# Bias tables, weight rounding and the split of h moved in a two-block transformer kernel

## What is computed

```python
h = h + rms_norm(ffn, g_ffn_post[i])
e = rms_norm(p[i] @ w_ple_proj[i], g_ple[i])
h = h + jax.nn.sigmoid(h @ w_ple_gate[i]) * e
```

## Time and profile before

| | |
|---|---|
| median of 3 runs | 2031.25 us |
| the profiled execution's own time | 2030.91 us |
| its span | 2028.9 us |
| PE busy (share of the span) | 1913.7 us (94%) |
| DVE, ACT, POOL busy | 50%, 36%, 37% |
| mean granted TensorE clock | 0.962 of full speed |

### The profile page before, as it was taken

One profiled execution on the slowest core, in us unless ns is written; L12 is line 12 of the kernel. 1 busy time (PEld: TensorE's weight loads), 2 busy tenths in 40 slices (PEclk: granted clock), 3 DMA queues, 4 the chain that ended last, 5 costly groups with the idle time before them and its releaser, 6 DMA issues.

```text
span 2028.9 us, 25065 instructions
## 1 busy us (share of the span) xinstructions
PE 1913.7 (94%) x9252; PEld 1556.2 (77%) x9252; DVE 1016.7 (50%) x1695; ACT 736.6 (36%) x1233; POOL 753.9 (37%) x319
## 2 busy tenths in 40 slices
PE   7689899999999799999999999999788899999997
PEld 6577587788888677788888888888655588888886
DVE  6964558634444644235443335631587635334444
ACT  5175653322223341133222223332388733222221
POOL 4132043444444334353455444544100035444542
PEclk9799999999999899999999999988789999999999
DMA  5112032233333223873333332333001123332321
GB/s 192 31 63 63 1 98 79 83 104 104 93 93 104 63 71 104 143 190 104 104 91 106 98 98 83 104 96 96 27 22 32 53 73 102 95 101 85 94 93 62
DMA packets 52235, 177.52 MB, mean 87 GB/s; under 512 B 5527, under 2 KB 5911, under 8 KB 52152
## 3 DMA queue, kind: packets, MB, share of 16 engines
q1 hardware_dynamic: 47952, 166.22, 26.4%
q10 hardware_dynamic: 4200, 10.15, 3.4%
HBM read 166.88 MB, written 9.47 MB: 87 GB/s over the span
## 4 chain that ended last, share of the span: by engine, by line
PE 78%; issue 9%; DVE 8%; ACT 2%; POOL 2%; DMA 0%; DVEq 0%; POOLq 0%; ACTq 0%
PE ps L401 24%; PE ps L403 24%; PE ps L402 24%; POOL WL L370 2%; DVE arena L1515 2%; DVE arena L2072 1%; DVE arena L2055 1%; PE ps L840 1%; PE ps L513 1%; PE ps L817 1%; PE ps L805 1%; ACT arena L1346 1%; ACT arena L993 0%; PE ps L831 0%; ACT arena L1352 0%
## 5 line engine op out<-in xcount | busy, mean ns | idle before, releaser
L370 POOL TENSOR_TENSOR WL<-raw,WH 128x1024 fp32r<-128x1024 f32 x295 | 735.8, 2509 | 1207.8 <-ACT WH L891 1207.8
L401 PE MATMUL ps<-XH,WH 128*128 128x512 f32 (+1 forms) x1280 | 504.6, 394 | 48.7 <-DVE arena L1499 16.8
L402 PE MATMUL ps<-XL,WH 128*128 128x512 f32 (+1 forms) x1280 | 502.1, 392 | 0.0
L891 ACT ACTIVATE WH<-raw 128x1024 fp32r<-128x1024 f32 x295 | 303.8, 1053 | 545.9 <-PE ps L403 487.6
L403 PE MATMUL ps<-XH,WL 128*128 128x512 f32 (+1 forms) x1280 | 501.8, 392 | 0.0
L401 PE MATMUL ps<-HH,WH 128*128 128x512 f32 x1072 | 420.5, 392 | 3.7 <-DVE HL L1786 3.7
L403 PE MATMUL ps<-HH,WL 128*128 128x512 f32 x1072 | 419.0, 391 | 0.0
L402 PE MATMUL ps<-HL,WH 128*128 128x512 f32 x1072 | 418.9, 391 | 0.0
L401 PEld LDWEIGHTS ps<-XH,WH 128*128 128x128 f32 x1280 | 248.9, 194 | 101.6 <-issue 41.1
L403 PEld LDWEIGHTS ps<-XH,WL 128*128 128x128 f32 x1280 | 248.9, 194 | 49.0
L402 PEld LDWEIGHTS ps<-XL,WH 128*128 128x128 f32 x1280 | 249.2, 195 | 48.1
(11 more groups left out here) (235 smaller groups left out, 1717.2 us busy)
## 6 DMA issues: line engine op xcount, KB each, us to landing
raw<-in_weights SPq DMA_DIRECT2D x301, 512.0 KB, 3.6
tab<-arena ACTq DMA_DIRECT2D x1, 5120.0 KB, 78.7
arena<-tab SPq DMA_DIRECT2D x16, 256.0 KB, 3.6
ftab<-arena ACTq DMA_DIRECT2D x1, 2080.0 KB, 23.4
h<-in_xT SPq DMA_DIRECT2D x8, 256.0 KB, 8.7
out_T<-h SPq DMA_DIRECT2D x8, 256.0 KB, 2.1
arena<-ftab ACTq DMA_DIRECT2D x4, 256.0 KB
arena<-in_pT ACTq DMA_DIRECT2D x1, 512.0 KB, 3.5
```

The lines of the kernel that those rows point to most:

```text
L370: nc.gpsimd.tensor_tensor(WL[:, s, :], raw[:, s, :], WH[:, s, :].bitcast(f32), SUB)\
L401: nc.tensor.matmul(out, wh, xh, start=start, stop=False)
L402: nc.tensor.matmul(out, wh, xl, start=False, stop=False)
L891: nc.scalar.activation(WH[:, s, :], raw[:, s, :], ACT.Copy).then_inc(*m["whi"].tick())
```

## The change

The bias tables' four products move from the mixer's turn j = 1 to the end of the FFN: two before `total(7, True)` and two after `spread()`. They now use banks 4, 5 and 6; the fourth waits until the first has been copied out. ACT copies them out instead of DVE: two copies before `XH[0]`, one after `XH[1]`, one after `XH[2]`. The two loads of their inputs move to the beginning of the FFN, and the buffers move within the arena.

ACT's rounding before `XH[1]` is taken away. Instead `upper(b.u + 3 + j)` rounds units 97 and 98 ahead of the squares of chunks 4 to 7, and `upper(b.u + 5)` rounds unit 99 ahead of the last square.

ACT and DVE split chunks 0 to 3 of `h` in the first half of the gate projection. In the second half DVE splits chunk c - 1 after it has updated chunk c.

```diff
--- before.py
+++ after.py
@@ -204,7 +204,7 @@
         act_, abs_, ay = cut(2564, 2, S), cut(3588, 2, S), cut(4612, 2, S)
 
-        ohs, relb, tabs, bcs = cut(12304, 1680), cut(13984, H2), cut(5636, 1680), cut(9728, GR, S)
+        ohs, relb, tabs, bcs = cut(14352, 1680), cut(16032, H2), cut(8192, 1680), cut(9728, GR, S)
 
         rt, st_ = cut(0, 4, S), cut(2048, 4, S)
 
@@ -570,17 +570,14 @@
                                                     skip_group_check=True)
                 last.then_inc(sems["v1_done"], 1)
 
-            def tables():
-
-                pe.wait_ge(sems["onehot_in"], 16)
-                pe.wait_ge(sems["relb_in"], 16)
-                for k in range(0, 1680, S):
-                    if k >= 2 * S:
-                        pe.wait_ge(*m["tab_out"].upto(k // S - 1))
-                    w = min(S, 1680 - k)
-                    nc.tensor.matmul(ps[0:H2, 4 + k // S % 2, 0:w], relb[0:33, 0:H2], ohs[0:33, k:k + w],
+            def tables(part):
+
+                for i in part:
+                    if i == 3:
+                        pe.wait_ge(*m["tab_out"].next())
+                    w = min(S, 1680 - S * i)
+                    nc.tensor.matmul(ps[0:H2, 4 + i % 3, 0:w], relb[0:33, 0:H2], ohs[0:33, S * i:S * i + w],
                                      start=True, stop=True).then_inc(*m["tab_done"].tick())
-                m["tab_out"].next(4)
 
             pe.wait_ge(sems["const_ok"], 2)
 
@@ -677,8 +674,12 @@
             project(2, 4, 2, XH, XL)
             down(0)
             down(1, True)
+            pe.wait_ge(sems["onehot_in"], 16)
+            pe.wait_ge(sems["relb_in"], 16)
+            tables((0, 1))
             total(7, True)
             spread()
+            tables((2, 3))
 
             for j in range(2):
@@ -693,8 +694,6 @@
                     total(7)
                 project(2, 4, 2, HH, HL, hooks={4: spread} if j == 0 else {})
                 project(2, 4, 2, HH, HL)
-                if j == 1:
-                    tables()
             for j in range(2):
                 project(4, 2, 4, XH, XL, m["x_lo"] if j == 0 else None)
             m["x_lo"].next(DC)
@@ -1152,6 +1151,8 @@
             ffn_up(2, 0, True)
             for c in range(DC):
                 square(c, ple[:, c, :], D)
+            act.dma_start(ohs[0:33, :], io["onehots"]).then_inc(sems["onehot_in"], 16)
+            act.dma_start(relb[0:33, :], io["relb"]).then_inc(sems["relb_in"], 16)
             upper(b.u + 3)
             lead = b.ahead - b.u
             with b.turns(act, 2, 24, dict(whi=24, tile_done=16, tile_free=32, ffn_g=8, ffn_gelu=8, hid_s=8, hid_hi=8)):
@@ -1165,19 +1166,27 @@
             down_rest(4, 2)
             nc.scalar.activation(small[:, 95:96], small[:, 0:1], ACT.Sqrt).then_inc(sems["warm"], 1)
             for j in range(2):
-                upper(b.u + 3)
+                upper(b.u + 3 + j)
                 for t in range(4):
+                    if j == 1 and t == 3:
+                        upper(b.u + 5)
                     act.wait_ge(*m["tile_free"].upto(t + 1))
                     square(4 * j + t, Y[:, 4 * j + t, :], D, 4 * j + t == DC - 1)
                 close(1, 4)
             root(D)
 
-
+            def copy_table(i):
+                w = min(S, 1680 - S * i)
+                act.wait_ge(*m["tab_done"].next())
+                nc.scalar.activation(tabs[0:H2, S * i:S * i + w], ps[0:H2, 4 + i % 3, 0:w], ACT.Copy).then_inc(*m["tab_out"].tick())
+
+            copy_table(0)
+            copy_table(1)
             for c in range(DC):
-                if c == 1:
-                    upper(b.u + 4)
                 act.wait_ge(*m["h_upd"].next())
                 nc.scalar.activation(XH[:, c, :], h[:, c, :], ACT.Copy).then_inc(*m["x_hi"].tick())
+                if c in (1, 2):
+                    copy_table(1 + c)
 
             def split_chunk(gain, c):
 
@@ -1185,24 +1194,20 @@
                     nc.scalar.activation(HH[:, c, :], h[:, c, :], ACT.Copy, scale=col(gain, c)).then_inc(*m["x_hi"].tick())
                 square(c, h[:, c, :], DC, gain is None and c == DC - 1)
 
-            for j in range(3):
-                if j < 2:
-                    upper(b.u + 4)
-                    upper(b.u + 7)
-                    for t in range(4):
-                        act.wait_ge(*landed(4, 4, t))
-                        nc.scalar.activation(ps[:, (b.t + t) % 4, :], ps[:, (b.t + t) % 4, :], ACT.Sigmoid)\
-                          .then_inc(*m["ple_s"].tick())
-                    close(4, 4)
-                if j >= 1:
-                    for t in range(4):
-                        act.wait_ge(*m["h_upd"].next())
-                        split_chunk("norm_mix_0", 4 * j - 4 + t)
+            for j in range(2):
+                upper(b.u + 4)
+                upper(b.u + 7)
+                for t in range(4):
+                    act.wait_ge(*landed(4, 4, t))
+                    nc.scalar.activation(ps[:, (b.t + t) % 4, :], ps[:, (b.t + t) % 4, :], ACT.Sigmoid)\
+                      .then_inc(*m["ple_s"].tick())
+                close(4, 4)
+                for t in range(4):
+                    act.wait_ge(*m["h_upd"].next())
+                    split_chunk("norm_mix_0", 4 * j + t)
             upper(b.u + 4)
             root(D)
             rstd_out()
-            act.dma_start(ohs[0:33, :], io["onehots"]).then_inc(sems["onehot_in"], 16)
-            act.dma_start(relb[0:33, :], io["relb"]).then_inc(sems["relb_in"], 16)
             act.dma_start(w2s, io["w2"]).then_inc(sems["w2_in"], 16)
 
@@ -1217,7 +1222,7 @@
                     nc.scalar.activation(XH[:, 2 * j + t, :], ay[:, t, :], ACT.Copy).then_inc(*m["x_hi"].tick())
                 close(2, 2)
                 if j == 1:
-                    act.wait_ge(*m["tab_out"].next(4))
+                    act.wait_ge(*m["tab_out"].upto())
                     act.dma_start(io["ftab"], tabs[0:H2, 640:].unsqueeze(1).to_broadcast([H2, 32, 1040]))\
                        .then_inc(sems["tab_st"], 16)
                     act.dma_start(io["tab"], tabs[0:H2, 0:640].unsqueeze(1).to_broadcast([H2, P, 640]))\
@@ -1788,32 +1793,26 @@
                 add_square(c, gain is None and c == DC - 1)
 
-            for j in range(3):
-                if j < 2:
-                    for t in range(4):
-                        c = 4 * j + t
-                        dve.wait_ge(*m["ple_s"].next())
-                        dve.wait_ge(*m["h_upd"].upto(-1))
-                        V.tensor_tensor(ptmp[:, t % 2, :], bank(t), ple[:, c, :], MUL).then_inc(*m["tile_free"].tick())
-                        dve.wait_ge(*m["tile_free"].upto())
-                        V.tensor_tensor(h[:, c, :], h[:, c, :], ptmp[:, t % 2, :], ADD).then_inc(*m["h_upd"].tick())
-                    close(4, 4)
-                    dve.wait_ge(*m["h_upd"].upto())
-                if j >= 1:
-                    for t in range(4):
-                        lower_chunk("norm_mix_0", 4 * j - 4 + t)
+            for j in range(2):
+                for t in range(4):
+                    c = 4 * j + t
+                    dve.wait_ge(*m["ple_s"].next())
+                    dve.wait_ge(*m["h_upd"].upto(-1))
+                    V.tensor_tensor(ptmp[:, t % 2, :], bank(t), ple[:, c, :], MUL).then_inc(*m["tile_free"].tick())
+                    dve.wait_ge(*m["tile_free"].upto())
+                    V.tensor_tensor(h[:, c, :], h[:, c, :], ptmp[:, t % 2, :], ADD).then_inc(*m["h_upd"].tick())
+                    if j and t:
+                        lower_chunk("norm_mix_0", c - 1)
+                close(4, 4)
+                dve.wait_ge(*m["h_upd"].upto())
+                for t in range(4) if j == 0 else (3,):
+                    lower_chunk("norm_mix_0", 4 * j + t)
 
             V.memset(apad[:, :, 0:2], 0.0).then_inc(*m["v_ok"].tick())
             invert()
             inverse()
             V.tensor_tensor(rr, rstd[:, :], rstd[:, :], MUL).then_inc(*m["r_ok"].tick())
             dve.wait_ge(*m["r_ok"].upto())
-
-            def copy_tables():
-                for k in range(0, 1680, S):
-                    w = min(S, 1680 - k)
-                    dve.wait_ge(*m["tab_done"].next())
-                    V.tensor_copy(tabs[0:H2, k:k + w], ps[0:H2, 4 + k // S % 2, 0:w]).then_inc(*m["tab_out"].tick())
 
             for j in range(4):
                 for t in range(2):
@@ -1852,8 +1851,6 @@
                     V.tensor_tensor(ay[:, t, :], act_[:, t, :], abs_[:, t, :], MUL).then_inc(*m["y_ok"].tick())
                 for t in range(2):
                     lower(XL[:, 2 * j + t, :], ay[:, t, :], XH[:, 2 * j + t, :], m["x_hi"], m["x_lo"])
-                if j == 1:
-                    copy_tables()
 
             def residual(n, nu, nt, gain):
 
```

## The result

| | before | after |
|---|---|---|
| median (4 runs each) | 2031.74 us (2031.1 to 2033.13) | 2020.45 us (2019.88 to 2021.8) |
| ratio after / before | | 0.9947, interval 0.9931 to 0.9963 |
| span of the profiled execution | 2028.9 us | 2018.9 us |
| PE busy in it | 1913.7 us | 1912.4 us |
| mean granted TensorE clock | 0.962 | 0.965 |

The change saves 11.3 us; 2020.9 was predicted. PE does the same work in both, so the gain is idle time and clock. The table follows one and the same operation of PE or ACT through both timelines; the last column says what each stretch gave. The first row compares distances from the start of two single executions, and is not as sharp as the others: in the eight traces whose kernels are the same up to there, the last product of unit 95 starts anywhere from 672.71 to 676.06.

The account below looks back on a forecast made before the run. PE bounds the kernel (78% of the chain), so its idle time and 1.2 GHz stretches can be won; 0.2 - 0.3 - 4.4 - 5.9 = -10.4 gives 2020.9 us for the median, range 2016.9 to 2024.1.

Parts of the forecast that it names:

- Loads at the beginning: FFN's beginning: two small DMAs issued on ACT delay the first subtraction; cost 0 to 0.5 us, taken as 0.2.
- Last squares: End of the FFN: total starts 3.1 us later, quicker update and earlier clock return follow; sum -0.3 us.
- worth 1.1: After the FFN's update: clock back at about 694, so 3 us of half rate instead of 5.3, worth 1.1 us.
- Early split: Mixer's start: PE goes straight on, with waits of 0.65 and 0.6 us in unit 105; -4.4 us.
- Tables: Mixer turn 1: 8.4 us of products, waits and half rate go; lost cushions at units 118 and 122 return 2.5: -5.9.
- 0.70 + 4.82 us: Mixer turn 1: time ACT needs to issue the table stores before it can round unit 118.
- From unit 132 on PE was dense before and stays so; nothing there gives it back: From unit 132 to the end: the gains made earlier all stay, so no term was set for it.
- Roundings pay as well: Last squares: POOL's subtraction of unit 99 queues after DVE's add, total starts at 677.9; 2017.6 us, chance 12%.
- The tables' products keep the clock up: End of the FFN: the moved products fill PE's gaps, so its clock doesn't fall; 2017.7 us, chance 12%.
- The store sets the pace: Mixer under the store: PE waits at units 118, 122 and 126, tables gain only 4.2 us; 2022.6 us, 12%.
- slower: Units 118 to 129: loads under the store fall further back, PE waits 12 us more; 2033 us, chance 3%.
- The split fails: Mixer's start: DVE stalls on `HH[4]`, PE waits 3 us in unit 105, clock falls; 2024.9 us, chance 7%.

Follow-up runs that it names:

- e3_round: The kernel before with only the roundings moved among the last squares: 2031.67 us, ratio 1.0004.
- e5_99late: The changed kernel with unit 99 rounded behind the last square, ahead of the root: 2016.97 us, ratio to before 0.9924.
- e6_early: As e5_99late, and units 97 and 98 rounded ahead of squares 0 and 4, one each: 2013.72 us, ratio 0.9916.
- after_again: The changed kernel once more, unaltered, on another chip as the measure for later variants: 2021.32 us, ratio 0.9951.
- e7_mixed: As e6_early, and ACT splits chunks 4 and 5 between the sigmoids instead of behind all four: 2015.15 us, ratio 0.9917.
- e2_tables: The kernel before with only the tables moved, with their loads, copies and buffers; roundings and split as before: 2026.3 us, ratio 0.9973.
- e1_split: The kernel before with only the early split of h: 2027.62 us, ratio 0.9983.

## Why the prediction was right, and where it was not

**Loads at the beginning** (+0.2): about +0.15. PE waits 3.21 us for the first subtraction instead of 3.06; it is 3.21 or 3.22 in all six traces with the loads moved and 3.04 to 3.06 in the eight others. The +0.29 at unit 95 has more in it that isn't the edit's: in this trace PE came to the wait 1.38 us later than before, and won it back behind it at a higher clock.

**Last squares** (-0.3): +0.31. The walk held: total at 680.37 (680.2 predicted), released by DVE behind three subtractions in turn with two adds; spread 4.5 us later than before; PE dense 1.01 us later, 0.72 of it in this stretch (+0.8). e3_round alone gives +0.73 at the same point, so it is the roundings, and e5 and e6 confirm that it is their place: with one subtraction out of the queue the last add falls from 2.23 to 0.68 us, with two, PE is dense 4.2 us earlier than in after_again. What failed is the term "worth 1.1" for an earlier return of the clock. It came back at 695.9, not at 694 (stretches of after):

```profile
694.00:695.00 1.00, 1.00 (x4) 0.81 (x3) 1.00 (x2) 0.48 (x1) 0.00 (x0) 0.50 0.00 0
695.00:696.00 1.00, 1.00 (x4) 0.76 (x4) 0.97 (x3) 0.15 (x1) 0.00 (x0) 0.65 0.00 0
696.00:697.00 1.00, 1.00 (x6) 0.82 (x5) 1.00 (x3) 0.50 (x1) 0.00 (x0) 1.00 0.00 0
```

That is 6.6 us after the product of 689.27, over the 3.8 to 6.3 that the prediction had counted; in e6_early it took 4.1 (684.86 to 688.91). The slow stretch of dense products is 4.7 us against 5.6, worth 0.4 us, not 1.1; in e3_round it was 3.9 us, worth 0.8. The term is real, but its size differs from trace to trace.

**Early split** (-4.4): -4.17, and -4.16 alone. (The prediction set its 747.8 against 752.22; the row of the total has 752.05, which makes its own term -4.25.) Both waits stand in unit 105, 0.47 and 0.30 us instead of 0.65 and 0.6, and the clock stays at 1.00. The total starts at 748.48 for 747.8 predicted, from a gate projection that ended 0.6 us later. e7_mixed shows that they can be taken away; in its five runs the 1.3 us don't reach the end.

**Tables** (-5.9): -8.55, and -8.55 alone, just outside the bound of -8.4. The products and the half rate behind them were 8.4, as predicted. The two waits did not come. The step that failed is "0.70 + 4.82 us" for the stores: the length of an issue was carried over from before, and it was 0.63. So ACT is free 4.19 us earlier than thought; `WL` of unit 118 comes 12.6 us earlier than before and that of unit 122 12.3, as much as PE (12.1), and both cushions are kept. Loads under the store did not fall back either.

**"From unit 132 on PE was dense before and stays so; nothing there gives it back"** failed. 3.1 us were given back between 1382 and 1459: 2.6 in products that ran longer at the lower clock, 0.5 in a wait for DVE of 6.12 us instead of 5.62. 1.0 was won again until the end, where I haven't followed it. Sum by the trace: 0.29 + 0.31 - 4.17 - 8.55 + 3.09 - 1.0 = -10.0, against -10.4 predicted. The forecast was right to half a microsecond because an error of -2.65 us (the tables), one of +0.6 (the clock) and +2.1 not foreseen nearly cancel; the mechanisms of three parts were right, the total was also luck. The stated range has a slip too: its lower end was said to be where two gains meet, but two gains of 3.3 and 3.2 us would meet at 2014.4, not at 2016.9.

The parts alone sum to -3.7, -5.0 and +0.4, -8.3 us, against -11.3 together (other chips and runs, each figure good to some 2 us). By the traces part of that is the clock again: e2_tables pays 3.9 us in the stretch in which e1_split pays nothing and after 2.6.

**The rivals.** *Roundings pay as well*: its condition did not occur, since POOL took unit 99 first; e5_99late makes it occur, and the stretch gains 1.4 us in its trace, not 3.3; the median is 4.35 us lower, of which the trace doesn't show the rest. *The tables' products keep the clock up*: no; in after the total runs its eight groups at 0.43 us each behind 3.8 us of idle, and in e2_tables, with the tables ahead and only 0.85 us idle, the groups slow down at 678.4 all the same. *The store sets the pace*, *slower*: no waits of PE at units 118 to 129. *The split fails*: `HH[4]` came at 736.94, no stall.

## What to carry to other kernels

Where VectorE adds SBUF tiles and GpSimd subtracts others, each such pair costs both; put the rounding that wakes GpSimd where VectorE reads PSUM or waits, one at a time: here that placement (e6_early) is worth 5.5 us in its own stretch on top of the change, and 7.6 in the medians, while the same roundings bunched were worth nothing (e3_round). Don't carry a duration of a DMA's issue over to another moment as if it were a property of the DMA: price it as a range; here the same store took 0.63 or 4.82 us. A gain of 12 us far up came out as 10 at the end, mostly because the clock fell at another place in a stage behind; a difference of 2 us in the end says little on an edit, the distance between two rows around it says much.

## What the hardware showed that I had not expected

- The issue of one and the same 5 MB store blocks ScalarE for 4.1 to 5.3 us or for 0.63 us; place, age and writer of its source change nothing.
- During 96 products of 48 columns, one every 0.11 us without a gap, TensorE's clock fell: 2.8 to 5.9 us after the first of them in all ten traces of the table. The 512-column products behind them ran at 1.2 GHz for another 2.9 to 5.9 us.
- Two kernels with the same instructions in a stretch of 70 us differ by up to 4.2 us there (70.5 to 74.7), while two executions of the changed kernel agreed to 0.02 us.
